# Block transposes on VectorE in a scan and in the experts, and a reordered projection stage, in a two-block network kernel

## The chip, the cores and the metric

The kernel runs on one core of a Trainium2 chip. The metric is the device time of one execution in microseconds (us); lower is better. Everything is float32. The instruction queues of TensorE (PE), ScalarE (ACT), VectorE (DVE), GpSimd (POOL, idle here) and SyncE (SP, which issues all DMAs) run side by side, each in order, and wait for each other by semaphores.

## What is computed

Two networks in a row on 256 tokens of width 1024, with 256 context tokens beside them. Cut to what the change touches:

```python
# first block, layer 0: an RWKV-7 scan over context and latent tokens, both directions
def step(S, inp):
    r_t, w_t, k_t, v_t, a_t, b_t = inp
    sa = jnp.einsum('bhvk,bhk->bhv', S, a_t)
    S = S * w_t[:, :, None, :] + sa[..., None] * b_t[:, :, None, :] + v_t[..., None] * k_t[:, :, None, :]
    return S, jnp.einsum('bhvk,bhk->bhv', S, r_t)

# first block, layer 1: 8 experts of width 2816, the best two for each token
for e in range(N_EXPERTS):
    out = out + gates[..., e:e + 1] * _swiglu(h, w1[e], w3[e], w2[e])

# second block, layer 0: gated short convolution beside differential attention
p = u @ w_in[j]                                  # gb, gc, v (512 each), q, k, v (512 each)
q, k = rope_2d(...), rope_2d(...); v = heads_v(p[..., V0:])
kvc = uc @ w_in[j][:, K0:]                       # the context's keys and values
o = diff_attention_blocks(q, concat([k, kc]), concat([v, vc]), lam)
y = jnp.concatenate([gb * short_conv(gc * v), sub_ln(o, subln_g[j], lam_init)], -1) @ w_out_mix[j]
```

The rest (Mamba scan, SwiGLU, neighbourhood attention, Fourier mixing, squared-ReLU MLPs, norms) is computed as well and is not changed.

## The kernel before, in words

The program is written engine by engine. Each engine's function lists its instructions in order; `did(engine, name)` counts a finished step on that engine's semaphore, and `at(engine, name)` gives the count that another engine waits for. So the order of the text in each function is the order of work. Weights come in slots of 256 columns through a ring of six (L500 issues each load when PE has finished the slot six before).

A float32 matmul of 128x128 by 128xN shows in the trace as two LDWEIGHTS and two MATMUL instructions. Line 928 is a helper, `two`, that issues two matmuls; 1618 is ACT's copy helper.

**The scan** (L884 to 1064 on PE, L1724 to 1772 on ACT, L2291 to 2428 on DVE) has 16 units: two directions, four chunks of 128 tokens, two groups of four heads. Each unit inverts, for each head, a triangular 128x128 matrix. `D0` holds its transposed 16x16 diagonal blocks (half 1 of the tile ED) and `E0` the same untransposed (half 0). PE squares them (E2, E4, E8), grows the inverse by T := T + T E (T2, T4, T8), and then joins blocks of 16 into 32, 64 and 128 by three bridges: Z = (masked matrix) T, then Tm = T + T Z. Powers and inverses are kept in both orientations, halves 0 and 1 of the tiles ED and TD, because a matmul wants its left operand transposed. PE computes each half by matmuls of its own; ACT copies the powers out of PSUM, 512 columns at a time; DVE adds to the inverse, 512 columns at a time (L2357 for T2, T4, T8, L2366 for the merges). `TT1` is the other half of the first inverse. The unit's other matmuls (decays, Gram products, transposes by token, outputs, state) of unit u+1 are placed between these steps. `decays(u)` on PE waits for DVE's `("state", u - 2)`, because ACT writes the exponentials `ex` that unit u - 2 still reads.

**The experts** (L1275 to 1396 on PE) run in blocks of one expert and up to 96 tokens; the table of blocks is worked out on the device, and 8 run with these inputs. A block gathers its tokens by a matmul with a one-hot matrix (L1282: 8 row tiles by 2 token chunks, 96 columns moving), giving them as 8 tiles of 128 features by 96 tokens. The up products (L1337) work in column tiles of 32: tokens are the stationary operand, three groups of 32, and the weights move, 4 parts of 352 columns of w1 or w3 into the 4 quarters of the partitions. ACT applies SiLU (L1889), DVE multiplies (L2638) into `hid`, [32 x 4 partitions, 352]. Since hidden feature 352 t + j lies in quarter t at column j, PE transposes each group in pieces of 128, 128 and 96 columns (L1321), ACT copies them out (L1894, L1895), and the down product (L1359) runs over 24 pieces of 128, 128 and 96 rows. Its weights w2 come in loads of 128 or 96 rows of 4 KB. Between its pieces PE adds the last block's outputs (L1293), turns the gates (L1379) and gathers the next block's tokens (L1282), which ACT copies out (L1868). A ring of 14 buffers carries all weights of the experts, 32 items of 704 KB (w1, w3) and 24 of 512 or 384 KB (w2) a block; SP issues item i (L597) when PE has used item i - 14.

**The second block's projections** (L1401 to 1446 on PE). After the experts come two norms, 4 and 5. Each norm is: DVE centres, ACT squares, PE sums over features by a matmul with a constant (L631), DVE adds epsilon, ACT takes the root, DVE divides and multiplies, ACT scales. Then `product` (L666) computes 16 tiles of gb, gc, v and q for the latent tokens, then four tiles of keys (L1426) for all 512 tokens, context and latent, and eight of values (L1438), each after a wait for ACT's copy of the one two before. PE turns q and k (L1415) for the rotary embedding, DVE applies it (L2674 to 2677).

**The attention** (L1448 to 1486, DVE L2682 to 2698) has eight units of a head and half of the queries. PE's order: scores of unit w+1, turned weights of w, values of w-1.

## Time and profile before

| | us |
|---|---|
| median of 3 runs | 3295.44 (3293.47 to 3298.66) |
| profiled execution, its own time | 3293.41 |
| its span | 3291.6 |
| PE busy | 3116.3 (95%) |
| DVE busy | 1283.0 (39%) |
| ACT busy | 588.3 (18%) |
| DMA | 551.15 MB, mean 167 GB/s |

The profiled execution's own time is 1.8 us more than its span, and 2.0 us less than the median. Busy times are unions over an engine's instructions. A stage can be bound by another engine than the whole, so the table is only a start: the rows below go stage by stage.

### The profile page before, as it was taken

Reading aid. Unit: us, or ns where it says so; the run is one execution under the profiler, and the core shown is the slowest. Engines: PE = TensorE matmul, PEld = TensorE weight load, DVE = VectorE, ACT = ScalarE, POOL = GpSimd, SP = SyncE. Lnnn points to the kernel's source line nnn. Section 1 sums busy time; section 2 is a strip of 40 time slices with the busy share of each in tenths; the row PEclk is TensorE's granted clock in tenths of the full one; section 3 lists DMA queues with packets and bytes.
Section 4 is the critical chain, followed back from the end, with each engine's and each line's share of the span. In section 5 each row is a group of like instructions: output and inputs, shape, how many; then the busy total and the mean of one; then the engine's idle time right before and its main releaser. Section 6 shows DMA issues by size and latency. Waiting matters only on the chain.

```text
span 3291.6 us, 52527 instructions
## 1 busy us (share of the span) xinstructions
PE 3116.3 (95%) x22488; PEld 2069.7 (63%) x22488; DVE 1283.0 (39%) x2836; ACT 588.3 (18%) x1314; POOL 0.2 (0%) x4
## 2 busy tenths in 40 slices
PE   7999899999999999999999999999999879988998
PEld 5454799997344443457745555445557568876887
DVE  1568666666799887503410101000112232122211
ACT  2114222222211111203310110010111220012000
POOL 0000000000000000000000000000000000000000
PEclk8999999999999999999999999999999889999999
DMA  7241001001577886330189999999984114531452
GB/s 264 75 154 51 1 1 40 1 1 39 189 239 243 245 248 187 123 99 25 70 317 362 357 339 337 343 362 367 349 231 130 51 52 141 153 115 51 133 148 64
DMA packets 351595, 551.15 MB, mean 167 GB/s; under 512 B 14512, under 2 KB 292400, under 8 KB 348048
## 3 DMA queue, kind: packets, MB, share of 16 engines
q1 hardware_dynamic: 351376, 547.89, 50.2%
q8 instruction: 178, 2.92, 0.4%
q14 instruction: 41, 0.34, 0.0%
HBM read 546.80 MB, written 1.05 MB: 166 GB/s over the span
## 4 chain that ended last, share of the span: by engine, by line
PE 89%; DVE 6%; ACT 2%; DMA 2%; issue 1%; SPq 0%; DVEq 0%; ACTq 0%
PE bank L666 15%; PE bank L1337 14%; PE bank L928 9%; PE bank L1130 8%; PE bank L1359 8%; PE bank L1517 7%; PE bank L1144 3%; PE bank L631 3%; PE bank L745 3%; PE bank L1171 2%; PE bank L1075 2%; DVE mix L2079 2%; PE bank L912 1%; PE bank L1282 1%; DMA arena<-in_ada_w 1%; PE bank L1426 1%
## 5 line engine op out<-in xcount | busy, mean ns | idle before, releaser
L666 PE MATMUL bank<-a,ring 128*128 128x256 f32 (+1 forms) x1792 | 454.8, 417 | 19.0 <-ACT a L1614 12.0
L666 PEld LDWEIGHTS bank<-a,ring 128*128 128x128 f32 x1792 | 344.9, 193 | 126.5 <-issue 74.5
L2079 DVE SCALAR_TENSOR_TENSOR mix<-arena,csil,mix 128x256 f32<-128x256 f32 x1008 | 402.0, 476 | 45.6 <-ACT mix L1618 45.6
L1337 PE MATMUL bank<-ring,arena 128*32 128x352 f32 x5376 | 406.9, 461 | 2.7 <-ACT small L1876 2.7
L1337 PEld LDWEIGHTS bank<-ring,arena 128*32 128x32 f32 x5376 | 175.1, 110 | 221.4 <-issue 220.4
L1130 PE MATMUL bank<-a,ring 128*128 128x512 f32 x704 | 307.5, 596 | 6.8 <-ACT a L1614 6.8
L1130 PEld LDWEIGHTS bank<-a,ring 128*128 128x128 f32 x704 | 133.2, 191 | 179.7 <-issue 178.0
L1517 PE MATMUL bank<-arena,ring 128*128 128x256 f32 x1024 | 223.5, 379 | 1.9 <-DVE arena L2736 1.9
L1618 ACT ACTIVATE arena<-bank 128x256 f32<-128x256 f32 (+1 forms) x303 | 142.0, 473 | 451.7 <-PE bank L928 199.2
L2638 DVE TENSOR_TENSOR arena<-arena,bank 128x352 f32<-128x352 f32 x48 | 25.0, 521 | 501.3 <-ACT arena L1889 501.3
L1359 PE MATMUL bank<-ring,arena 128*32 128x256 f32 (+1 forms) x3840 | 219.0, 380 | 0.6 <-issue 0.6
L1517 PEld LDWEIGHTS bank<-arena,ring 128*128 128x128 f32 x1024 | 194.4, 190 | 29.1 <-DVE arena L2736 2.8
L928 PE MATMUL bank<-arena 128*128 128x128 f32 x1408 | 180.6, 281 | 3.1 <-DVE arena L2344 2.1
L928 PEld LDWEIGHTS bank<-arena 128*128 128x128 f32 x1408 | 166.4, 193 | 14.6 <-ACT arena L1618 6.7
L1359 PEld LDWEIGHTS bank<-ring,arena 128*32 128x32 f32 (+1 forms) x3840 | 121.9, 110 | 83.5 <-issue 9.5
L1144 PE MATMUL bank<-arena,ring 128*128 128x512 f32 x352 | 154.1, 597 | 2.1 <-DVE arena L2460 2.1
L2717 DVE TENSOR_SCALAR tmpA<-bank,mods 128x256 f32<-128x256 f32 x32 | 15.5, 484 | 288.4 <-PE bank L1517 213.9
L1144 PEld LDWEIGHTS bank<-arena,ring 128*128 128x128 f32 x352 | 67.5, 192 | 88.4 <-issue 85.5
L1567 ACT ACTIVATE mix<-a 128x256 f32<-128x256 f32 x64 | 21.8, 417 | 534.1 <-DVE a L1994 534.1
L1618 ACT ACTIVATE mix<-arena,csil 128x256 f32<-128x256 f32 x144 | 64.7, 499 | 261.6 <-DMA arena<-in_ada_w 160.6
L745 PE MATMUL bank<-a,ring 128*128 128x512 f32 (+1 forms) x224 | 99.1, 596 | 0.0
L2732 DVE TENSOR_SCALAR tmpA<-bank 128x256 f32<-128x256 f32 x64 | 27.2, 424 | 167.1 <-PE bank L666 167.1
(411 smaller groups left out, 3360.6 us busy)
## 6 DMA issues: line engine op xcount, KB each, us to landing
ring<-in_moe_w SPq DMA_DIRECT2D x224, 704.0 KB, 8.4
ring<-in_mlp_w SPq DMA_DIRECT2D x64, 1024.0 KB, 5.5
ring<-in_moe_w SPq DMA_DIRECT2D x112, 512.0 KB, 8.4
arena<-in_ada_w SPq DMA_DIRECT2D x96, 512.0 KB, 3.8
arena<-in_w_ada SPq DMA_DIRECT2D x48, 512.0 KB, 3.6
ring<-in_ffn_w SPq DMA_DIRECT2D x22, 1024.0 KB, 8.5
arena<-in_moe_w SPq DMA_DIRECT2D x32, 704.0 KB, 8.8
ring<-in_moe_w SPq DMA_DIRECT2D x48, 384.0 KB, 8.4
```

The source lines that it names most:

```text
L631: i = mm(bank[b][:, 0:tile.shape[-1]], const("mean"), tile, start=(k == 0), stop=(k == KT - 1))
L666: i = mm(bank[b][:, 0:n], ws[:, k, t * P:t * P + P], rhs[:, k, sl], start=(k == 0), stop=(k == KT - 1))
L745: i = mm(bank[RKV_BANK[n]][0:m, :], ws[:, k, n % 2 * P:n % 2 * P + m], aT[:, k, :], start=(k == 0), stop=(k == KT - 1), skip_group_check=True)
L928: i = mm(bank[b][:, o + P * m:o + P * m + P], lhs[:, m, :], rhs[:, m, :], start=True, stop=True, skip_group_check=True)
L1075: i = mm(bank[MIX_BANKS[j % 5]], ws[:, k, j % 2 * P:j % 2 * P + P], src, start=(k == 4), stop=(k == 3), skip_group_check=True)
L1130: i = mm(bank[2 * t + i_], ws[:, k, t * P:t * P + P], aT[:, k, :], start=(k == 0), stop=(k == KT - 1))
L1144: i = mm(bank[2 + n % 4], ws[:, k, :], G[:, k, :], start=(k == 0), stop=(k == FT - 1))
L1337: i = mm(b[32 * t:32 * t + 32, 0:PART], ac_[:, k, 32 * g:32 * g + 32], ws[i_][:, PART * t:PART * t + PART], start=(k == 0), stop=(k == KT ...
L1359: i = mm(bank[Y_BANKS[g]][32 * q:32 * q + 32, 0:256], gT[0:rows_, p, g, o + 32 * t:o + 32 * t + 32], ws[0:rows_, 256 * q:256 * q + 256], s ...
L1517: j = mm(bank[4 + n % 2][:, 0:TL], ws[:, k, :], G2[:, 16 * half + k, :], start=(half + k == 0), stop=(half * k == 15))
L1618: act(dst, src, ACT.Copy, scale=scale).then_inc(act_done, did(AC, name))
L2079: ins = V.scalar_tensor_tensor(dst, x, cond, dst, ALU.mult, ALU.add)
```

## The change

It touches four stages.

1. In the scan, PE computes half 0 only of E2 and E4 (the powers), of T2, T4, T8 and of the first merge. DVE makes half 1 by a transpose in blocks of 32x32 (`V.transpose`), which for matrices that are zero outside their 32x32 diagonal blocks is the whole transpose. The second merge makes both halves, the third half 1, as before. `TT1` goes. The wait of `decays` for the state moves from PE to ACT and is for `("state 1", u - 2)`. DVE's order of the products, masks and additions changes.
2. In the experts, the columns of w1 and w3 are dealt to the four quarters in runs of 32: quarter t takes columns 128 c + 32 t + j. Then a 32x32 block transpose of `hid` by DVE gives features 128 c to 128 c + 127 on the partitions, and the down product has 22 pieces of 128 rows (`DOWN`). The gather puts tokens on partitions in quarters, with the features moving in runs of 32 as well, and DVE block-transposes it into `ac_`. PE's transposes of `hid` and ACT's copies of them and of the gather go. The ring has 54 items a block; the first 12 items of a block wait for the item 12 before them, not 14.
3. After the experts, the context's keys and values are computed by PE before, between and after the two norm sums of stage 5; the weights of keys and values are the first four slots (`kv2`). The latent ones follow, then gc, v, q, gb.
4. In the attention, scores run two units ahead, and the product with gb follows in DVE's first units.

```diff
-PIECES = ((0, 128), (128, 128), (256, 96))
-BLOCKS_AT = [(p, t, i) for p in range(2) for t in range(4) for i in range(3)]
-ITEMS = 32 + len(BLOCKS_AT)
+DOWN = [(p, c) for p in range(2) for c in range(PART // 32)]
+ITEMS = 32 + len(DOWN)
+def uses(i):
+    return len(range(i % MRING, ITEMS, MRING))
...
-    add("in2", w["w_in_2"][0], 0, KT, by(0, 3072))
+    add("kv2", w["w_in_2"][0], 0, KT, by(2048, 1024))
+    add("in2", w["w_in_2"][0], 0, KT, by(512, 1536) + by(0, 512))
...
-                            prev = (i - MRING) % ITEMS
+                            prev = i - MRING if i >= MRING else i + MRING * (uses(i) - 1)
...
# PE, scan
             def decays(u):
-                if u >= 2:
-                    pe.wait_ge(vec_done, at(VE, ("state", u - 2)))
...
             def grams(u):
                 pe.wait_ge(act_done, at(AC, ("bkt", u)))
+                pe.wait_ge(vec_done, at(VE, ("ar r", u)))
...
+            def squared(name, u, p, i):
+                two(POWER_BANK[p], 0, half_of(ED, i, p, 1), half_of(ED, i, p, 0)
+                    ).then_inc(pe_done, did(PE, (name, u, p)))
+            def grown(name, u, p, by, i, halves=(0,)):
+                t_ = half_of(TD, i, p, 0)
+                for half in halves:
+                    ins = two(GROW_BANK[p], 256 * half, *((t_, by) if half else (by, t_)))
...
+                grown(("Tm", lv), u, p, z, 1 - lv % 2, ((0,), (0, 1), (1,))[lv])
...
                     grown("T2", u, p, half_of(ED, 1, p, 0), 0)
+                    pe.wait_ge(vec_done, at(VE, ("E2 turned", u, p)))
                     squared("E4", u, p, 1)
...
                     grown("T4", u, p, half_of(ED, 0, p, 0), 1)
+                    pe.wait_ge(vec_done, at(VE, ("E4 turned", u, p)))
+                    squared("E8", u, p, 0)
...
# PE, experts
+            def by_tile(x, t):
+                return x.rearrange("p (c t j) -> p c t j", t=4, j=32)[:, :, t, :]
             def gather():
+                for g in range(GROUPS_OF):
                     for c in range(2):
+                        for q in range(4):
+                            i = mm(bank[4 * (g // 2)][32 * q:32 * q + 32, 256 * (g % 2):256 * (g % 2) + 256],
+                                   pm[:, c, 32 * g:32 * g + 32], by_tile(atok[:, c, :], q),
+                                   start=(c == 0), stop=(c == 1), skip_group_check=True)
...
-                                    i = mm(b[32 * t:32 * t + 32, 0:PART], ac_[:, k, 32 * g:32 * g + 32],
-                                           ws[i_][:, PART * t:PART * t + PART], start=(k == 0),
+                                    i = mm(b[32 * t:32 * t + 32, 0:PART], ac_[:, g, 32 * k:32 * k + 32],
+                                           by_tile(ws[i_], t), start=(k == 0),
...
+                for n, (p, c) in enumerate(DOWN):
...
+                                   gT[:, p, g, 32 * c:32 * c + 32],
+                                   ws[:, 256 * q:256 * q + 256], start=(n == 0),
...
# PE, second block
+            pe.wait_ge(act_done, at(AC, ("norm", 13, KT - 1, 0)))
+            context_keys(0)
+            context_keys(1)
             mean_after(5, 4)
+            context_keys(2)
             squares_in(5, LAT)
+            context_keys(3)
+            context_values(0)
+            context_values(1)
...
             scores2(0)
+            scores2(1)
             for w_ in range(len(DIFF_UNITS)):
+                if w_ + 2 < len(DIFF_UNITS):
+                    scores2(w_ + 2)
...
# ACT
             def decays(u):
+                if u >= 2:
+                    ac.wait_ge(vec_done, at(VE, ("state 1", u - 2)))
...
+                    copy((name, u, p), ED[i][:, p, 0:256], bank[POWER_BANK[p]][:, 0:256])
...
# DVE
+            def power_turned(name, u, p, i):
+                ve.wait_ge(act_done, at(AC, (name, u, p)))
+                V.transpose(ED[i][:, p, 256:512], ED[i][:, p, 0:256]
+                            ).then_inc(vec_done, did(VE, (name + " turned", u, p)))
             def grown(name, u, p, i, before):
+                V.tensor_tensor(TD[1 - i][:, p, 0:256], TD[i][:, p, 0:256], bank[GROW_BANK[p]][:, 0:256], ALU.add
...
+            def inverse_turned(name, u, p, i, before):
+                ve.wait_ge(vec_done, before)
+                V.transpose(TD[i][:, p, 256:512], TD[i][:, p, 0:256]).then_inc(vec_done, did(VE, name))
...
+                grown("T2", u, 0, 0, at(VE, ("T1", u)))
+                power_turned("E4", u, 0, 0)
...
+                grown("T4", u, 0, 1, at(VE, ("T2", u, 0)))
+                grown("T4", u, 1, 1, at(VE, ("T2", u, 1)))
...
+                    inverse_turned(("T8 turned", u, p), u, p, 1, at(VE, ("T8", u, p)))
...
+                    inverse_turned(("Tm turned", u, 0, p), u, p, 0, at(VE, ("Tm", u, 0, p)))
...
+            def gathered(g, inc, counter, name):
+                V.transpose(ac_[:, g, :], bank[4 * (g // 2)][:, 256 * (g % 2):256 * (g % 2) + 256]
+                            ).then_inc(inc, did(counter, (name, g)))
...
+                def hidden_turned(p, g):
+                    ve.wait_ge(ve_moe, e * per + at(VEM, ("hid", p, g)))
+                    V.transpose(gT[:, p, g, :], hid[:, p, g, :]).then_inc(ve_moe, did(VEM, ("gT", p, g)))
...
+                if 1 <= w_ < 5:
+                    gated_conv(w_ - 1)
```

## Rows read from the trace of the kernel before

**Rows 1.** The page's chain that ended last, by engine.

```profile
PE 89%; DVE 6%; ACT 2%; DMA 2%; issue 1%; SPq 0%; DVEq 0%; ACTq 0%
```

**Rows 2.** Windows: span, busy per engine (instructions), PE clock, DMA share, GB/s.

```profile
346.00:795.00 449.00, 437.10 (x3657) 411.42 (x3658) 285.94 (x543) 123.30 (x298) 0.00 (x0) 1.00 0.03 11
1857.00:1957.00 100.00, 100.00 (x1468) 51.72 (x1460) 8.40 (x22) 10.02 (x26) 0.00 (x0) 1.00 1.01 352
...
2600.00:2650.00 50.00, 30.38 (x128) 21.33 (x128) 19.37 (x45) 21.17 (x59) 0.00 (x0) 0.76 0.07 21
```

**Rows 3.** Windows: one unit of the scan (PE, PEld, DVE, ACT, POOL).

```profile
374.00:402.00 28.00, 27.19 (x231) 25.55 (x230) 18.28 (x35) 7.80 (x19) 0.00 (x0) 1.00 0.00 1
```

**Rows 4.** Timeline of the scan: start, us, engine, line, operation, shapes.

```profile
455.46 0.68 DVE L2340 TENSOR_TENSOR arena<-arena,consts 128x512 f32<-128x512 f32 x1
...
456.66 0.87 DVE L2366 TENSOR_TENSOR ring<-arena,bank 128x256 f32<-128x256 f32 x2 [0.52 <-PE bank L928]
...
457.44 0.68 DVE L2344 TENSOR_TENSOR arena<-arena,consts 128x512 f32<-128x512 f32 x1
...
465.64 0.69 DVE L2357 TENSOR_TENSOR arena<-ring,bank 128x512 f32<-128x512 f32 x1 [2.22 <-PE bank L928]
...
467.02 3.65 PEld L928 LDWEIGHTS bank<-arena 128*128 128x128 f32 x32
```

**Rows 5.** Waits in the scan: who for whom, us in total, times, longest.

```profile
PE bank L891 <- DVE ring L2424: 5.8, 8, 0.7
...
PE bank L891 <- DVE ring L2426: 4.3, 6, 0.7
```

**Rows 6.** Timeline of norm 4: DVE's reciprocal.

```profile
2465.26 1.75 DVE L2009 RECIPROCAL tmpA<-tmpB 128x256 f32<-128x256 f32 x1 [0.48 <-ACT tmpB L1580]
```

**Rows 7.** Chain of waits in the experts: start, us, what, instructions.

```profile
1698.44 0.48 PE bank L1321 x3
...
1745.80 3.74 PE bank L1282 x32
1749.54 9.21 PE bank L1359 x168
1758.75 39.05 PE bank L1337 x528
...
1957.47 2.64 PE bank L1337 x33
```

**Rows 8.** Windows: w2 alone loading, then w1 and w3 alone; DMA share, GB/s last.

```profile
1920.00:1940.00 20.00, 20.00 (x354) 12.21 (x350) 3.23 (x8) 1.50 (x6) 0.00 (x0) 1.00 1.02 287
1950.00:1990.00 40.00, 40.00 (x584) 18.91 (x580) 2.04 (x5) 3.61 (x7) 0.00 (x0) 1.00 1.01 406
```

**Rows 9.** DMA issues from 1920 to 1940: count, size, median us to landing.

```profile
ring<-in_moe_w SPq DMA_DIRECT2D x4, 512.0 KB, 8.7
ring<-in_moe_w SPq DMA_DIRECT2D x2, 384.0 KB, 8.3
```

**Rows 10.** Waits of SP's queue in the experts.

```profile
SPq L597 <- PE bank L1337: 351.8, 128, 22.3
```

**Rows 11.** Chain of waits from norm 4 to the last values.

```profile
2460.51 3.73 PE bank L631 x16
...
2468.07 6.25 PE bank L631 x16
...
2585.57 13.83 PE bank L1438 x64
2599.43 0.38 ACT arena L1618
```

**Rows 12.** Chain of waits over one unit of the attention.

```profile
2620.91 1.29 DVE small L2685 x2
...
2623.37 1.12 PE bank L737 x4
...
2627.62 1.29 DVE small L2685 x2
```

More of the change, by code:

```diff
@@ new lines, in context_values @@
+            def context_values(c):
+                for half in range(2):
+                    ws = full(first["kv2"] + 2 + half)
+                    for k in range(KT):
+                        i = mm(bank[5 - c][:, 256 * half:256 * half + 256], aT[:, k, c * P:c * P + P],
+                               ws[:, k, :], start=(k == 0), stop=(k == KT - 1), skip_group_check=True)
+                i.then_inc(pe_done, did(PE, ("v2 ctx", c)))
+            pe.wait_ge(act_done, at(AC, ("norm", 13, KT - 1, 0)))
@@ L1416, in turn @@
                    ).then_inc(pe_done, did(PE, ("turn", n)))
[L1418 to L1419 removed]
+            for j in range(4):
+                s = first["kv2"] + j // 2
                 ws = full(s)
[L1421 to L1429 removed]
@@ L1430, in _ @@
[L1430 to L1443 removed]
+                if j >= 2:
+                    pe.wait_ge(act_done, at(AC, ("k2", j - 2)))
@@ new lines, in _ @@
+                for k in range(KT):
+                    if j == 0:
+                        normed(5, k)
+                    i = mm(bank[2 + j % 2][:, 0:TL], ws[:, k, j % 2 * P:j % 2 * P + P], aT[:, k, LAT],
+                           start=(k == 0), stop=(k == KT - 1))
+                i.then_inc(pe_done, did(PE, ("k2", j), *([("slot", s)] if j % 2 else [])))
+            for n in range(4):
+                half, c = n // 2, 2 + n % 2
+                s = first["kv2"] + 2 + half
+                ws = full(s)
+                pe.wait_ge(act_done, at(AC, ("v2 ctx", n) if n < 2 else ("v2", n - 2)))
+                for k in range(KT):
+                    i = mm(bank[5 - n % 2][:, 0:256], aT[:, k, c * P:c * P + P], ws[:, k, :],
+                           start=(k == 0), stop=(k == KT - 1))
+                i.then_inc(pe_done, did(PE, ("v2", n), *([("slot", s)] if c == 3 else [])))
+                turn(n)
@@ L1444, in _ @@
+            pe.wait_ge(act_done, at(AC, ("k2", 3)))
+            product("in2", first["in2"], 8, aT, LAT, [2, 3],
+                    lambda j: pe.wait_ge(act_done, at(AC, ("in2", j))),
+                    then=lambda j: turn(j - 4) if 8 <= j < 12 else None)
+            pe.wait_ge(act_done, at(AC, ("in2", 15)))
             pe.wait_ge(vec_done, at(VE, ("rope", 7)))
-            pe.wait_ge(act_done, at(AC, ("v2", 7)))
             def scores2(w_):
```

266 lines of the change are left out of this document (110 added, 156 removed).

## The prediction

> **What bounds it now.** I read the chain of waits first: PE's work makes 89% of it [rows 1], so what counts is where PE is busy, and whether it would stay busy with less to do. The table of stages answers by stage [rows 2]. In the RWKV scan (346 to 795 us) PE is busy 437 of 449 us while DVE is busy 286: PE-bound. In a middle stretch of the experts it is busy 100 of 100 us, but the DMA share is 1.01 too, so two resources are full and taking work from one may show the other. In the attention of the second block (2600 to 2650) PE is busy 30 of 50 us at a granted clock of 0.76: a chain of waits, not work. The profiled execution took 3293.4 us, 2.0 under the median of the three runs shown; the sums below go against it, and 2 us are added at the end.
>
> **The scan.** One unit takes 28.0 us, with PE busy 27.2 of them [rows 3]; there are 16. The change keeps only one orientation of most small inverses on PE and lets DVE turn it in 32x32 blocks. Per unit it drops these 128x128 matmuls: E2 4, E4 4, T2, T4 and T8 4 each, first merge 4; 24 in all. Each is two instructions in the trace, and 32 instructions in a row take 3.65 us [rows 4], 0.114 each; 48 x 0.114 = 5.5 us a unit, -87.5 us over 16. The decays no longer wait for the state of u-2 on PE (ACT waits for the earlier "state 1" instead); that wait is 5.8 + 4.3 us [rows 5]: -10.
>
> What DVE gets: 8 transposes of 128x256 a unit. No row shows one. Its lower bound is nothing (a transpose cannot free DVE); for the upper I take the slowest 128x256 operation of DVE, the reciprocal at 1.75 us [rows 6]. I take 0.45, nearest to the 128x256 additions, which write as many elements (0.87 us for two) [rows 4]. DVE also gives back: six additions and two merges shrink from 512 to 256 columns (0.69 to 0.43, 2.1 us) and the 512-wide "TT1" goes (0.7). So DVE gets 3.6 and loses 2.8 us: some 18.7 busy in a unit of 22, and ACT's four 512-wide copies become 256 wide. The reordered products of DVE (bh and kh first, then ar) have the same work; the Gram products now also wait for "ar r", which is issued after both T4 additions and before T8: about 0.1 us more. The chain of each step gets longer while PE has less to fill it: T2's addition plus E4's transpose on DVE is about 0.9 us against two pairs of PE products of 0.45 each, so T4 of the second pair comes 0.1 to 0.2 late. The three bridges wait for ACT as before. I add 0.3 us a unit, +5. Sum of the scan -93; a unit of about 22.1 us. With transposes at 0.9 us, 8 x (0.9 - 0.6) comes onto the unit, since beyond about 0.6 each one lies on the chain: then the scan gives -64.
>
> **The experts.** There are 8 blocks, the second and third taking (1957.47 - 1758.75) / 2 = 99.4 us each [rows 7]. Off PE in each: six groups of transposes of the hidden values at 0.48 = 2.9 us; two of the 24 pieces of the down product, since 96-row pieces go (seven pieces take 9.21, so 1.32 each): 2.6; the gather goes from 3.74 us to 24 matmuls of 256 columns in four column tiles, which is what two down pieces are, 2.6: 1.1 less [rows 7]. Together 6.6 us a block; PE alone would want 92.8. DVE gets nine transposes a block beside 8.4 us of work in 100 [rows 2]: hidden, with PE's own products as cover (the last is wanted 11 pieces later). ACT loses its copies. The first block starts later, since its three transposes follow "blocks" on DVE: +1.
>
> The moving operand of all up products is now read in 11 runs of 32 columns, 512 bytes apart. No row of PE shows such a read. On DVE, a read in four runs of 128 columns costs 0.68 us (L2340), as the unbroken L2344 does [rows 4]. I take nothing; the bound above is half the rate, which is a rival below. The page Advanced Engine Details and Errata of the Trainium skill (Memory Cachelines) gives SBUF lines of 16 bytes and no penalty within one, which a run of 128 bytes keeps; its rule that any non-contiguous pattern slows matmuls significantly is about PSUM, which the change still writes contiguously.
>
> But the DMA: while only w2 is loaded it moves 287 GB/s at a share of 1.02, and while only w1 and w3 are, 406 at 1.01 [rows 8]. A block needs 32 x 721 KB = 23.1 MB and 11.5 MB, so 56.8 + 40.2 = 97.0 us if these rates are the DMA's own. If w2's time goes by transfers and not by bytes, 22 for 24, it is 56.8 + 36.8 = 93.6. For the latter speaks that 384 KB take as long to land as 512 KB (8.3 and 8.7) [rows 9]; against a DMA bound, that SP waited 352 us for the up products to free slots [rows 10]. I take 94.2, so 5.2 a block and -42 in all; ends 92.8 and 97.0, -53 and -19. The page DMA: Bandwidth & Descriptors of the Trainium skill (Specifications) gives about 358 GB/s of HBM for a core, and a block of 34.6 MB would take 96.7 us by it; the 406 GB/s over 40 us speak against that as a limit here.
>
> **The second block's projections.** From the norm sum of stage 4 (2460.51 + 3.73 = 2464.2) to the end of v2 (2599.43) are 135.2 us [rows 11]. PE's work in them is that of two norm sums (2 x 3.45), and, at the 13.83 us that v2 takes for 64 instructions, 55.3 for in2's 256 and 27.7 each for keys and values, eight turns, two instructions each (3.5): 121.1. The change moves no work off PE; it puts the context's half of keys and values, 27.7 us, into the gaps between the norms, with its weights as the first four slots, of which six 1 MB loads begin when the experts end. The norms themselves then come some 3 us later, but behind them lie 17 us of keys and values that need none of them. So the stage becomes pure PE work, 14.1 shorter; a stretch at the lower clock of 1.2 GHz, which before took 6.25 us for 16 instructions [rows 11], will probably cost some 2 us somewhere: -12 (-8 to -14). The gated product with gb moves behind the scores; DVE has the room.
>
> **The attention.** A unit takes 2627.62 - 2620.91 = 6.7 us, all in series: DVE's maxima, ratio and weights 2.5 us, then PE's turn, values and the next scores, 4.2 us from 2623.37 [rows 12]. With scores two ahead, the scores and maxima leave that chain. What remains is the larger of PE's own 4.2, most of it at the lower clock (half of it at the full one), and ACT's and DVE's 2.5 to 3; I take 4.7 with its waits. Over seven periods, -14 (-8 to -17).
>
> **Sum.** -93 - 42 + 1 - 12 - 14 = -160: 3133.4, and on the median 3135.
>
> **Rivals.**
> **DMA-bound experts**: blocks of 97.0 us instead of 94.2 give back 8 x 2.8 = 22: 3157. For it, the share of 1.01; against, SP's waits for PE. 20%.
> **Slow transposes**: at 1.3 us instead of 0.45, DVE's chain adds 8 x 0.7 = 5.6 us to a unit, 90 in all: 3225; at 1.75 the whole scan gives nothing. 8%.
> **Moving runs, the other side**: the four column tiles make 192 quad passes a block, at 0.296 us each (39.05 us for 528 instructions, 132 passes) [rows 7], 1536 in all. If a run of 32 columns makes PE read at half rate, each takes 0.30 more: +450, some 3585. It decides from 160 / 1536 = 0.10 us more a pass, 35%: then the change is slower than before. By the PSUM rule above, were it true of moving reads, it would come out here; nothing in the trace speaks for it. 7%.
> **Latency under the PE work**: the scan does not follow its work, since the chain of products, ACT copies and DVE additions already took 28 us. Then only the experts, the projections and the attention gain: 3228. Against it, DVE waited for PE and not the reverse, and PE idles only 0.8 us of a unit [rows 3]. 5%.
> My forecast, with its pieces a little off: 60%.
>
> **The numbers.** Predicted 3135. Below, all ends at their best (-96, -53, -14, -17) give 3116, with a little for a faster clock in the attention 3108. Above, the DMA-bound case and transposes near 0.9 give 3135 + 22 + 29 = 3186; I stop at 3190 and leave out the slow transposes beyond that, the latency and the moving runs. Under 0.2%, about 7 us, a measurement cannot tell a change from none. Faster 0.91, the same 0.02, slower 0.07, from the moving-runs case.
>
> **What would show it.** A scan unit near 22 us with PE still busy over 95% (else the chain is the bound), a transpose row near 0.45 us; up products still at 39 us for 528 instructions; blocks of 93 to 95 us, and PE waits for a DMA in the experts if the DMA is the bound; no idle of PE between 2464 and the scores; attention units under 5 us. The forecast is wrong if the up products' passes take over 0.31 us, or if the scan's unit stays over 24.

## The result and the profile after

The kernel after takes **3103.97 us** (median of 4 runs, 3100.58 to 3104.77), the kernel before on the same chip 3294.99 (3293.47 to 3298.66): a ratio of 0.9417, 95% interval 0.9400 to 0.9433. The change gives 191 us where the prediction said 160. The direction was right; the time lies 4 us below the low end of the range (3108). So the prediction is wrong in size, and the question is which terms were too small.

The profiled execution took 3104.1 us, its span 3102.3. Cut at the same places in the chain of waits of both kernels (start of the up products of the first block, end of the experts' last down piece, end of the projections, start of the output product), the 189.3 us between the spans are:

| stage | before | after | difference | forecast |
|---|---|---|---|---|
| up to the experts' start | 1657.63 | 1562.16 | -95.5 | -93 + 1 |
| eight blocks of experts | 798.0 | 736.9 | -61.0 | -42 |
| norms and projections | 143.8 | 129.6 | -14.2 | -12 |
| attention | 54.9 | 33.6 | -21.2 | -14 |
| the rest | 637.3 | 639.9 | +2.6 | 0 |

The two terms that are off are the experts' (19 us) and the attention's (7 us).

**The scan.** A window of the kernel after, as long as a unit (columns: stretch, its length, busy time and instructions of PE, PEld, DVE, ACT and POOL, granted clock, DMA share, GB/s; against [rows 3]):

```profile
374.00:396.00 22.00, 21.92 (x184) 20.36 (x183) 18.22 (x42) 6.92 (x19) 0.00 (x0) 1.00 0.00 1
```

and two of its three groups of DVE's block transposes in the scan (count, busy us, mean ns, then the idle time before them; the third, 32 of the inverse in other buffers, has 445 ns):

```profile
L2357 DVE STREAM_TRANSPOSE arena<-arena 128x256 f32<-128x256 f32 x64 | 28.3, 443 | 12.6 <-ACT arena L1628 12.3
L2370 DVE STREAM_TRANSPOSE arena<-arena 128x256 f32<-128x256 f32 x32 | 14.3, 446 | 1.1
```

A transpose takes 0.44 us (0.45 was taken), and a unit 22.0 us (22.1 was forecast). What the reader should see is PE at 21.92 of 22.00: the unit is still nothing but PE's work, and DVE, to which the transposes went, has 18.2 us of work in a unit, as before.

**The experts.** The chain of waits of the kernel after through one block (start, duration, what; it stands against [rows 7]):

```profile
1656.59 56.80 PE bank L1336 x768
1713.39 10.36 PE bank L1352 x192
1723.75 2.80 PE bank L1295 x48
1726.56 9.20 PE bank L1352 x168
...
1736.56 2.73 PE bank L1352 x48
1739.29 2.59 PE bank L1284 x48
1741.88 6.47 PE bank L1352 x120
1748.36 56.80 PE bank L1336 x768
```

A block takes 1748.36 - 1656.59 = 91.77 us, all PE, where the forecast had 94.2 and its floor, PE alone, 92.8. The DMA did not hold it up. Its windows after, the whole stretch in which only rows of w2 move and a stretch in which only w1 and w3 do, and its landings of w2 (KB each, median us from issue to landing), against [rows 8, 9]:

```profile
1791.00:1823.00 32.00, 32.00 (x520) 17.47 (x516) 6.12 (x14) 1.39 (x3) 0.00 (x0) 1.00 0.91 344
1842.00:1862.00 20.00, 20.00 (x276) 8.78 (x272) 0.00 (x0) 0.42 (x1) 0.00 (x0) 1.00 1.02 418
```
```profile
ring<-in_moe_w SPq DMA_DIRECT2D x160, 512.0 KB, 6.6
```

w1 and w3 come at the old rate (418 GB/s, 406 before). w2 comes at 344 GB/s where the prediction read 287, and at a lower share, 0.91 for 1.02. The window of that reading holds the ends of w1 and w3 as well, by some 5% of its rows; over the whole stretch in which only rows of w2 moved, the kernel before had this:

```profile
1899.00:1937.00 38.00, 38.00 (x579) 19.83 (x575) 4.79 (x11) 4.12 (x13) 0.00 (x0) 1.00 1.01 276
```

That is the surprise: the same weights, from the same place, a quarter faster, and nothing in the change was seen as touching their rate. By the new rates a block's weights need 23.1 MB / 418 GB/s + 11.5 MB / 344 GB/s = 55.2 + 33.5 = 88.7 us (an estimate from these windows), 3 us less than PE's 91.8.

**The projections.** The chain after: from the norm sum (L634) to the end of gb (L669) PE's pieces follow each other without a gap.

```profile
2304.11 3.72 PE bank L634 x16
2307.83 6.91 PE bank L1395 x32
...
2328.55 13.81 PE bank L1405 x64
...
2418.34 10.37 PE bank L669 x48
```

Its window, with PE busy all but 0.1 us and the granted clock at 1.00:

```profile
2304.00:2428.00 124.00, 123.89 (x574) 109.04 (x575) 31.48 (x75) 25.97 (x62) 0.00 (x0) 1.00 0.42 135
```

**The attention.** One steady unit of the chain after, and the start of the next, against [rows 12]:

```profile
2444.74 0.66 PE bank L740 x4
2445.39 0.89 PE bank L1481 x8
2446.29 1.06 PE bank L1462 x4
...
2447.38 0.66 PE bank L740 x4
```

A unit takes 2447.38 - 2444.74 = 2.64 us, all PE. It took 6.7 before, and 4.7 was forecast. PE's three pieces, turn, values and scores, are 2.6 us here and were 1.12 + 1.71 + 1.40 = 4.2 before. The granted clock (third column from the right) was 0.76 there [rows 2]; here it is low only in the first units, behind 6 us (2428 to 2434) of which PE was busy 4.0:

```profile
2434.00:2442.00 8.00, 7.86 (x28) 4.42 (x27) 6.06 (x14) 4.47 (x13) 0.00 (x0) 0.57 0.00 0
2442.00:2450.00 8.00, 7.66 (x49) 4.88 (x49) 7.52 (x17) 6.62 (x22) 0.00 (x0) 1.00 0.00 1
```

So these are the same instructions at the upper clock of 2.4 GHz instead of mostly at the lower one.

### The profile page after: what moved, and what is told of

The parts are those of the page before. It is cut to its first block, busy times and chain, and to the rows that moved or that the text cites. A ratio compares the mean times of both kernels' runs of the same rounds, so it can differ in the third digit from the quotient of the medians.

```text
span 3102.3 us, 50418 instructions
## 1 busy us (share of the span) xinstructions
PE 2959.7 (95%) x21400; PEld 1945.2 (63%) x21400; DVE 1316.5 (42%) x3023; ACT 539.0 (17%) x1200; POOL 0.2 (0%) x4
## 4 chain that ended last, share of the span: by engine, by line
PE 90%; DVE 5%; ACT 2%; DMA 2%; issue 1%; SPq 0%; DVEq 0%; ACTq 0%
PE bank L669 16%; PE bank L1336 15%; PE bank L1128 9%; PE bank L1352 7%; PE bank L1527 7%; PE bank L930 7%; PE bank L1142 4%; PE bank L634 3%; PE bank L748 3%; PE bank L1169 2%; PE bank L1073 2%; DVE mix L2083 2%; PE bank L914 1%; DMA arena<-in_ada_w 1%; PE bank L1203 1%; PE bank L1295 1%
## 5 line engine op out<-in xcount | busy, mean ns | idle before, releaser
L669 PE MATMUL bank<-a,ring 128*128 128x256 f32 (+1 forms) x1792 | 453.4, 415 | 15.4 <-ACT a L1624 8.3
L669 PEld LDWEIGHTS bank<-a,ring 128*128 128x128 f32 x1792 | 343.6, 193 | 121.9 <-issue 70.2
L1336 PEld LDWEIGHTS bank<-ring,arena 128*32 128x32 f32 x5376 | 176.4, 110 | 227.9 <-issue 226.9
L1352 PE MATMUL bank<-ring,arena 128*32 128x256 f32 x3840 | 213.3, 379 | 0.0
L1628 ACT ACTIVATE arena<-bank 128x256 f32<-128x256 f32 (+1 forms) x303 | 127.7, 428 | 371.6 <-PE bank L930 137.3
L1352 PEld LDWEIGHTS bank<-ring,arena 128*32 128x32 f32 x3840 | 124.2, 110 | 83.4 <-issue 4.0
L930 PE MATMUL bank<-arena 128*128 128x128 f32 x896 | 125.4, 285 | 3.9 <-DVE arena L2350 2.1
L930 PEld LDWEIGHTS bank<-arena 128*128 128x128 f32 x896 | 110.1, 193 | 16.5 <-ACT arena L1628 7.7
L748 PE MATMUL bank<-a,ring 128*128 128x512 f32 (+1 forms) x224 | 99.6, 599 | 0.0
```

What stands on the lines that cost most here:

```text
L669: i = mm(bank[b][:, 0:n], ws[:, k, t * P:t * P + P], rhs[:, k, sl], start=(k == 0), stop=(k == KT - 1))
L748: i = mm(bank[RKV_BANK[n]][0:m, :], ws[:, k, n % 2 * P:n % 2 * P + m], aT[:, k, :], start=(k == 0), stop=(k == KT - 1), skip_group_check=True)
L930: i = mm(bank[b][:, o + P * m:o + P * m + P], lhs[:, m, :], rhs[:, m, :], start=True, stop=True, skip_group_check=True)
L1336: i = mm(b[32 * t:32 * t + 32, 0:PART], ac_[:, g, 32 * k:32 * k + 32], by_tile(ws[i_], t), start=(k == 0), stop=(k == KT - 1), skip_group_ ...
L1352: i = mm(bank[Y_BANKS[g]][32 * q:32 * q + 32, 0:256], gT[:, p, g, 32 * c:32 * c + 32], ws[:, 256 * q:256 * q + 256], start=(n == 0), stop= ...
L1628: act(dst, src, ACT.Copy, scale=scale).then_inc(act_done, did(AC, name))
```

## The experiments

### Each part alone

Four kernels, each the kernel before with one of the four parts of the change and nothing else. Their cores:

```diff
# scan alone
-                    ins = two(POWER_BANK[p], 256, e, d_)
+                V.transpose(ED[i][:, p, 256:512], ED[i][:, p, 0:256]
# experts alone
-PIECES = ((0, 128), (128, 128), (256, 96))
+DOWN = [(p, c) for p in range(2) for c in range(PART // 32)]
# projections alone
+            context_keys(0)
+            context_keys(1)
             mean_after(5, 4)
# attention alone
             scores2(0)
+            scores2(1)
```

> The kernel before with the scan's part of the change alone. By the stages of the two traces the scan gave 96.6 us. If the parts are independent this gives -95 to -98 against before, ratio 0.970 to 0.971. If the scan's gain owes something to the other parts (the clock, say), less. My forecast for the term was -93.

> The kernel before with the experts' part alone. The stages gave -61.1 in the experts and +1.1 before them; forecast -42, with ends -53 and -19. If the parts are independent: -58 to -62, ratio about 0.982, blocks of 91.8 us. If the experts' extra gain came from elsewhere (the scan or the projections feeding the weights' queue), -42 to -53 and blocks of 93 to 94.

> The kernel before with the second block's projections reordered alone. The stages gave -14.1; forecast -12 (-8 to -14). Independent parts: -12 to -15. Rival: the product with gb, moved into the attention, costs there when scores run only one unit ahead: then -6 to -10. Nothing else should move.

> The kernel before with the scores of the attention two units ahead, alone. The stages gave -21.2; forecast -14 (-8 to -17), with units of 4.7 us. After the change the units take 2.65 us at the full clock. Theory one, the clock came back because the scores ahead keep PE busy: then -19 to -22 here too. Theory two, the full clock came from the unbroken PE work of the projections ahead of it: then only -12 to -17 here, with units of 4 to 5 us at a granted clock under 0.9.

| run | median us | ratio to before (95%) | against 3297.15 |
|---|---|---|---|
| scan alone | 3198.96 | 0.9697 (0.9671 to 0.9722) | -98.2 |
| experts alone | 3237.35 | 0.9814 (0.9788 to 0.9841) | -59.8 |
| projections alone | 3283.58 | 0.9960 (0.9940 to 0.9980) | -13.6 |
| attention alone | 3269.88 | 0.9912 (0.9886 to 0.9938) | -27.3 |

The kernel before ran from 3291.9 to 3311.0 in this job, so each difference is good to some 8 us. They add up to 199, the change to 191: the parts are independent within that. The experts' gain is their own, with the landing of w2 at 6.5 us in that kernel too, so neither the scan nor the other order of slots made w2 faster.

The attention's 27.3 against the 21.2 of its stage lies within that. Its trace tells which theory holds. Between 2600 and 2650 us, where the kernel before has PE busy 30.38 us at a clock of 0.76 [rows 2], it shows:

```profile
2600.00:2650.00 50.00, 42.11 (x207) 30.40 (x206) 22.98 (x53) 23.14 (x64) 0.00 (x0) 0.90 0.07 22
```

and its chain has a unit of 2.55 us:

```profile
2619.59 0.59 PE bank L737 x4
...
2622.14 0.62 PE bank L737 x4
```

The stage, from the end of v2 to the output product, takes 2640.12 - 2607.72 = 32.4 us, 22.5 less than before. The projections ahead of it are the old ones here, and in the projections alone, whose PE work runs into the attention without a gap, the units keep the old pieces (1.12, 1.71 and 1.2 to 1.5 us). So the clock came back because scores two ahead keep PE busy in the attention, as theory one said, not because of what runs ahead of it.

### The wait of the decays

```diff
             def decays(u):
-                if u >= 2:
-                    pe.wait_ge(vec_done, at(VE, ("state", u - 2)))
-                elif u == 0:
+                if u == 0:
# ACT, before it writes the exponentials
+                if u >= 2:
+                    ac.wait_ge(vec_done, at(VE, ("state 1", u - 2)))
```

> The kernel before, with only the wait of the decays for the state of u-2 taken from PE, and ACT waiting for the earlier state 1 of u-2 before it writes the exponentials. My term for it was -10: the 5.8 and 4.3 us that PE waited for DVE there. If that wait is worth its length, -8 to -10, ratio about 0.997. Rival: the steps behind it wait instead (for the bridges' masks and copies), since PE gets to them earlier: then -2 to +2, and the whole -96 of the scan is from the fewer matmuls.

It takes 3282.59 us, ratio 0.9957 (0.9941 to 0.9972): 13.9 us less. The rows of the decays' line in the kernel before, in this one, in the one with doubled transposes (next section) and in the kernel after, in that order, give the scan's pace (duration min/median/max, then start of the first and last instruction, one set of four a unit):

```profile
L891 PE MATMUL bank<-consts,ring x64: 381/381/576, 332.4 to 748.4; 128*128 128x258 f32 x64
```
```profile
L889 PE MATMUL bank<-consts,ring x64: 381/381/639, 335.0 to 737.5; 128*128 128x258 f32 x64
```
```profile
L892 PE MATMUL bank<-consts,ring x64: 381/381/639, 335.6 to 690.2; 128*128 128x258 f32 x64
```
```profile
L892 PE MATMUL bank<-consts,ring x64: 381/381/639, 333.9 to 661.9; 128*128 128x258 f32 x64
```

The decays of unit u+1 open unit u, so from the first to the last lie the scan's opening and fourteen whole units: 416.0, 402.5, 354.6 and 328.0 us. PE's busy time in these stretches, of the kernel before, of this one and of the kernel after:

```profile
332.40:748.40 416.00, 397.77 (x3300) 372.37 (x3301) 265.15 (x507) 112.44 (x274) 0.00 (x0) 0.98 0.03 9
```
```profile
335.00:737.50 402.50, 394.43 (x3299) 371.26 (x3300) 265.13 (x507) 112.38 (x273) 0.00 (x0) 0.99 0.03 9
```
```profile
333.90:661.90 328.00, 320.61 (x2620) 296.43 (x2621) 267.35 (x608) 99.99 (x273) 0.00 (x0) 0.98 0.03 11
```

The wait was worth 13.5 us: PE idles 10.2 us less, the wait's own length, and the same matmuls take 3.3 us less, at a mean granted clock of 0.99 for 0.98. Nothing took its place, and the rival is out. The other 402.5 - 328.0 = 74.5 us are the matmuls that were dropped: PE is busy 73.8 us less, 5.3 a unit, and its idle time went from 8.1 to 7.4. So the transposes put no wait in PE's way that shows here, where the prediction had set 5 us aside.

### Each transpose twice

```diff
                 ve.wait_ge(vec_done, before)
+                op(("once", name), V.transpose(TD[i][:, p, 256:512], TD[i][:, p, 0:256]))
                 V.transpose(TD[i][:, p, 256:512], TD[i][:, p, 0:256]).then_inc(vec_done, did(VE, name))
```

and the same for the powers.

> The kernel after, with each of the scan's eight block transposes a unit done twice, one after the other (0.44 us each in the profile after). It measures how much room the chain of a unit has under PE's work. My prediction held that a transpose has about 0.6 us before it lies on the chain, and 0.9 us would cost 8 x 0.3 = 2.4 us a unit, +38 us. A model of the unit with each engine's queue in order gives 23.7 us for a unit of 22.0, +27. If PE's work covers the transposes well: under +10. DVE's busy time goes from 18.2 to 21.7 us a unit, so DVE itself is then nearly full.

3133.81 us (3129.17 to 3137.72) against 3103.40 for the kernel after in the same job: +30, of which the rows above show 354.6 - 328.0 = 26.6 in fourteen units, 1.9 a unit. Eight more transposes are 8 x 0.446 = 3.6 us a unit, so half of their time comes onto the path. The model of the queues (+27) came close, the rule of the prediction (room up to 0.6 us, then all of it, +38) was too harsh. The waits of PE in this kernel show where (us in total, times, longest):

```profile
PE bank L930 <- DVE ring L2372: 7.7, 16, 0.5
PE bank L930 <- DVE arena L2365: 6.7, 15, 1.3
```

L2372 is the transpose of the inverse after T8 or the first merge, L2365 the addition to the inverse. In the kernel after, the same view shows one PE wait of 0.6 us for that addition (L2364) and one of 0.4 for that transpose (L2370) in all of the scan: a transpose of 0.44 us just fits.

### The moving operand in runs of 32

```diff
-                                           by_tile(ws[i_], t), start=(k == 0),
+                                           ws[i_][:, PART * t:PART * t + PART], start=(k == 0),
```

> The kernel after, with the moving operand of the up products read in one run of 352 columns, as before, instead of 11 runs of 32 (hidden features land in other places, so the values differ). If runs of 32 columns cost nothing, the up products of a block stay at 56.8 us (768 instructions) and the whole within 3 us of after. If they cost something, the block falls by it: 0.01 us a pass would be 1.9 us a block and 15 us in all.

3097.15 us in one run. The up products and the block, from its chain:

```profile
1745.33 56.80 PE bank L1336 x768
...
1837.09 7.97 PE bank L1336 x105
```

56.80 us for 768 instructions and a block of 91.76, both the same to 0.01 us as with runs of 32. Moving runs of 32 float32 columns, 512 bytes apart, cost nothing, and almost all of the 7 us between the two totals lies ahead of and behind the experts, in the spread of single runs (the kernel after itself ran from 3096.85 to 3106.20 in another job).

### Why w2 became faster

Three kernels for three theories: the loads of 96 rows slow the whole stream (A), it is where the rows start (B), or the rate is that of the bytes and bounds the block (C). The kernels of this section and the next read other rows of w2 than the network wants or leave old ones in the slots, so they show times only, and each is one run. In the kernel before:

```diff
-                                f0 = MCOLS * p + PART * t + o
-                                src = w["moe_w2"][0][one, f0:f0 + n, :]
-                                dst = dst[0:n, 0:D]
+                                f0 = MCOLS * p + PART * t + o + n - P
+                                src = w["moe_w2"][0][one, f0:f0 + P, :]
+                                dst = dst[:, 0:D]
```

> The kernel before, with every load of w2 128 rows long: where it read the last 96 rows of a piece, it now reads the 128 rows that end there (the down product of that piece still multiplies 96 partitions, with values of other rows). w2's bytes grow by 9%. Before, w2's loads took 8.4 us from issue to landing, and while only they ran the DMA share was 1.02 at 287 GB/s; after the change 6.6 us, 0.85 and 317 GB/s. Theory A, the 96-row loads slow the whole stream of w2: landings fall to about 6.6 to 7 us, the share in a w2-only window to 0.9 or less at 310 GB/s or more. Theory B, it is where the rows start (before at multiples of 32 rows, after at multiples of 128): landings stay at 8.4 us or grow, share 1.0. Theory C, the rate is that of the bytes, and the DMA bounds the block: the block grows from 99.4 us to 102 or more. By A and B, PE bounds the block before: it stays at 99.4 us, and the whole within 5 us of before.

In the kernel after, with loads of 96 rows back, 6 of 22 where 8 of 24 were, and with all loads shifted:

```diff
-                                src = w["moe_w2"][0][one, f0:f0 + P, :]
-                                dst = dst[:, 0:D]
+                                n = 96 if c % 3 == 2 else P
+                                src = w["moe_w2"][0][one, f0:f0 + n, :]
+                                dst = dst[0:n, 0:D]
# the shifted one
-                                f0 = MCOLS * p + P * c
+                                f0 = MCOLS * p + P * c + (32 if c < 10 else 0)
```

> The kernel after, with every third load of w2 96 rows instead of 128 (the last 32 rows of those slots keep what lay there; the products are as many). PE's work is unchanged, w2's bytes fall by 8%. Theory A (96-row loads slow the stream): landings of w2 rise from 6.6 to 8 us or more and the share in a w2-only window from 0.85 to 0.95 or more, with fewer bytes moved. Whether the block of 91.8 us grows is open: if the DMA then needs more than that, it goes to 93 to 95. Theory B (the start of the rows): landings stay at 6.6 us and the share falls to about 0.8.

> The kernel after, with w2's rows read 32 rows later (still 128 rows a load; ten of eleven loads multiply other rows than they should). Theory A (96-row loads): as after, landings 6.6 us, share 0.85, block 91.8 us. Theory B (loads that start at a multiple of 128 rows, 512 KB, are faster): landings 8 us or more, share 0.95 or more.

3294.43 us (before, all loads 128 rows), **3126.51** (after, every third load 96 rows) and 3105.45 (after, shifted). The stretches in which only rows of w2 move, and the landings, first of the kernel before with 128 rows:

```profile
1899.00:1938.00 39.00, 39.00 (x593) 20.34 (x587) 4.79 (x11) 4.27 (x14) 0.00 (x0) 1.00 0.87 303
```
```profile
ring<-in_moe_w SPq DMA_DIRECT2D x160, 512.0 KB, 5.5
```

then of the kernel after with every third load 96 rows:

```profile
1794.00:1826.00 32.00, 32.00 (x531) 19.70 (x527) 6.12 (x14) 1.39 (x3) 0.00 (x0) 1.00 1.03 259
```
```profile
ring<-in_moe_w SPq DMA_DIRECT2D x120, 512.0 KB, 20.0
ring<-in_moe_w SPq DMA_DIRECT2D x40, 384.0 KB, 20.0
```

Theory A holds from both sides. With 9% more bytes, the kernel before moves w2 at 303 GB/s instead of 276, at a share of 0.87 instead of 1.01, and lands a load in 5.5 us instead of 8.4. With 7% fewer bytes, the kernel after moves it at 259 instead of 344, and lands a load in 20.0 us instead of 6.6. B is out: shifted rows land in 6.6 us and cost nothing. C, the byte rate as the bound, is out as well, since the larger w2 left the block at 99.4 us.

The second of the three is also what the prediction's reading would have looked like in time. Its chain has the loads in it (the time of an entry is a load's whole flight, not a wait), here in the fifth block, between the start of the first up products and the end of the last down piece:

```profile
1560.58 59.50 PE bank L1337 x768
...
1983.82 23.13 DMA ring<-in_moe_w
...
2318.04 6.52 PE bank L1353 x120
```

From 1655 to 2243 us PE is busy 573.5 of 588 us there, and all 588 in the kernel after. The eight blocks take 2324.56 - 1560.58 = 764.0 us where the kernel after takes 736.9: 27 us more, of which the whole shows 22 (the stretches outside differ by 5, within the spread of single runs). The loss grows as the lead of the ring is used up. From one start of the up products to the next are 94.4, 92.8, 94.1, 94.0, 99.3, 96.4 and 96.2 us (94.3 and then 91.8 or 91.9 in the kernel after), and the last four blocks take 97.2 on the mean. By this kernel's own rates a block needs 10.7 MB / 259 GB/s + 23.1 MB / 418 GB/s = 96.7 us (an estimate). So the sum of the two rates is what a block takes once the DMA is the bound: the prediction's 97.0, and not the 94.2 that it took.

### What makes a short load slow

```diff
+                                n = 64 if c % 3 == 2 else P      # or 112; or n = 96 for all
```

> The kernel after, with every third load of w2 64 rows instead of 128. With 96 rows there the time went from 3104 to 3126.5 us, the w2-only window from 317 GB/s at a share of 0.85 to 265 at 1.03, and 512 KB took 20.0 us to land instead of 6.6. Theory P, 96 rows are slow because they don't divide evenly (six rows for each of the 16 DMA engines, where 128 rows give eight and 64 give four): with 64 rows the time stays within 3 us of 3104, the share in a w2-only window at 0.7 to 0.8, landings near 6.6 us. Theory Q, any mixture of lengths disturbs the stream, or any load under 128 rows is slow: 3115 us or more, landings over 10 us, share over 0.95.

> The kernel after, with every third load of w2 112 rows (seven for each DMA engine). Theory P: slow as with 96, 3115 us or more, landings over 10 us. Theory Q with the loss growing with what is missing from 128: about half of the 22 us of 96 rows, 3110 to 3118. If 112 rows cost nothing (3104, landings 6.6), it is 96 alone that is slow.

> The kernel after, with every load of w2 96 rows. The bytes of w2 fall to three quarters. If a load of 96 rows is slow by itself (P), the stream stays slow: 3115 us or more, the w2-only window under 270 GB/s at a share over 1. If it is the alternation of 96 and 128 that is slow (part of Q), it recovers: 3104 us, the w2-only window at a share of 0.65 to 0.8 and landings under 6.6 us.

| w2 in the kernel after | whole, us | eight blocks | GB/s, share | one row |
|---|---|---|---|---|
| all 128 rows | 3103.97 | 736.9 | 344, 0.91 | 0.17 us |
| every third 64 | 3105.06 | 741.0 | 264, 1.03 | 0.26 |
| every third 96 | 3126.51 | 764.0 | 259, 1.03 | 0.26 |
| every third 112 | 3146.87 | 779.6 | 270, 1.03 | 0.25 |
| all 96 | 3105.93 | 745.5 | 247, 1.02 | 0.27 |

The eight blocks are cut as in the table of stages. The rates are of the stretches in which only rows of w2 move: 1791 to 1823, 1790 to 1822, 1794 to 1826, 1805 to 1833 and 1790 to 1822 us. The last column is an estimate of how long one of the 16 DMA engines is busy with a row of 4 KB: the share times 16 times the stretch, over the packets of 512 B and more. (The expectations quote shorter windows, 317 GB/s at 0.85 for all 128 rows and 265 at 1.03 for every third 96.) Two of the windows, 112 and all 96:

```profile
1805.00:1833.00 28.00, 24.62 (x412) 14.04 (x408) 6.12 (x14) 1.39 (x3) 0.00 (x0) 1.00 1.03 270
```
```profile
1790.00:1822.00 32.00, 31.53 (x511) 18.91 (x507) 6.13 (x14) 1.39 (x3) 0.00 (x0) 1.00 1.02 247
```

and the packets of the first row of the table and of the third:

```profile
DMA packets 3015, 11.00 MB, mean 344 GB/s; under 512 B 341, under 2 KB 341, under 8 KB 3011
```
```profile
DMA packets 2282, 8.30 MB, mean 259 GB/s; under 512 B 269, under 2 KB 269, under 8 KB 2278
```

Neither theory comes out. P had 64 rows harmless: the whole is unchanged, but the share is 1.03, the landings are 9.9 us and the blocks take 4 us more. Q had all 96 recover: the rate stays at 247 GB/s, and the whole hardly moves because a quarter of the bytes is gone (the blocks take 9 us more even so). What the runs do show is simpler and enough for the case. With full loads alone a row takes a DMA engine 0.91 x 16 x 32 / 2674 = 0.17 us; as soon as 64, 96 or 112 rows stand in every third load, or 96 in all, it takes 0.25 to 0.27 on the mean. The rows of the full loads are among the slow ones: with every third load 96 rows, 22% of the rows belong to short loads, but the median of all rows from 1650 to 2290 us, in the trace's own records of packets, is 0.236 us, and 0.159 in the kernel after. The kernel before fits as well, with 0.24 us a row and 0.19 once all its loads have 128 rows. So leaving out 32 rows of every third load, or even 16, costs 22 and 43 us. The page DMA: Bandwidth & Descriptors of the Trainium skill (Why a DMA increments its semaphore by 16 and not by 1) says that 96 rows are spread over as many of the DMA engines, 16, as 128; a full share with 96 rows agrees with that, and so the loss isn't from idle engines. Why each row gets slower is left open, and so is why 112 rows cost more than 96 at about the same rate.

### The first block earlier

An attempt at a faster version. In the trace after, the first gather ends on PE at 1557.2 us, but DVE turns the tokens only behind its small operations:

```profile
1552.02 5.20 PE L1284 MATMUL bank<-arena 128*32 128x256 f32 x48 [1.33 <-DVE arena L2592]
1560.60 1.11 DVE L2634 STREAM_TRANSPOSE arena<-bank 128x256 f32<-128x256 f32 x3
1562.16 4.33 PE L1336 MATMUL bank<-ring,arena 128*32 128x352 f32 x28 [4.94 <-DVE small L2642]
```

```diff
# DVE: ahead of the operations that lead to "blocks", not behind them
+            ve.wait_ge(pe_done, at(PE, "gather first"))
+            for g in range(GROUPS_OF):
+                gathered(g, vec_done, VE, "gathered first")
+            ve.wait_ge(vec_done, now(VE))
+            V.memset(small[:, 701:702], 0.0).then_inc(ve_moe, per)
             which4 = which.rearrange("p i (m e) -> p i m e", m=2)
# ACT: releases the block before it waits for "blocks"
-            act(small[:, 700:701], small[:, 604:605], ACT.Copy).then_inc(ac_moe, per)
+            act(small[:, 700:701], small[:, 32:33], ACT.Copy).then_inc(ac_moe, per)
+            ac.wait_ge(vec_done, at(VE, "blocks"))
```

> The kernel after, with the first block of experts let go earlier. In the trace after, the first gather ends on PE at 1557.2 us, but DVE turns it only at 1560.6, behind the small operations that work out which experts need a second block, and PE starts the up products at 1562.2. None of those small operations is needed by the first block's up products. Here DVE turns the gathered tokens ahead of them, right when the gather ends, and releases PE and ACT then. Expected: the up products start at 1558.6, 3.5 us earlier, and the whole is 3 to 4 us faster (ratio to after 0.9989). Rivals: ACT, which must now load its table and wait for the number of blocks, is late for the first SiLU (it is wanted 27 us later, so no); or the later small operations delay the first mask of gathered tokens (wanted at the end of the block, so no): then nothing is gained.

> The kernel after once more, beside the next one on the same chip: 3100 to 3105 us.

```profile
1550.25 4.48 PE L1284 MATMUL bank<-arena 128*32 128x256 f32 x48 [1.32 <-ACT a L1624]
1555.30 1.11 DVE L2617 STREAM_TRANSPOSE arena<-bank 128x256 f32<-128x256 f32 x3
1556.87 9.59 PE L1336 MATMUL bank<-ring,arena 128*32 128x352 f32 x104 [2.13 <-DVE small L2625]
```

From the start of the gather to the first up product are 10.1 us in the kernel after and 6.6 here: 3.5 less, as expected. The runs took 3097.66 us (3097.32 to 3101.34) against 3103.40 (3096.85 to 3106.20). Their ratios to before, 0.9400 (0.9388 to 0.9413) and 0.9407 (0.9394 to 0.9420), overlap, so of the 5.7 us between the medians only the 3.5 in the trace is shown. (A second trace of the kernel after has the same 10.1 us, from 1553.10 to 1563.24.)

## Why the prediction was right in direction and wrong in size

- **The scan, -93 and measured -96.6** (95.5 to the experts' start, with 1.1 given back there). The count of dropped matmuls held, a transpose cost 0.44 us, and PE stayed at 99.6% of a unit. The size is partly luck, since three terms were off and nearly cancelled: the dropped matmuls gave 5.3 us a unit, some 84 in all, for 87.5 (the price of 0.114 was read from a row of weight loads); the decays' wait gave 13.5 for 10; and the 5 us set aside for new waits were not needed. Two slips in the working decide nothing here: DVE's terms add up to 19.1 us a unit and not 18.7 (measured 18.2), and transposes at 0.9 us cost 38 us by the rule given, so that the scan would have given -55 and not -64, and the upper sum 3195.
- **The experts, -42 and measured -61.0.** This is the step that failed: "if these rates are the DMA's own". I took 287 GB/s at a full share for w2's rate, and so 94.2 us a block, between PE's own 92.8 and 97.0 by the two rates. The rate belonged to a stream with 96-row loads in it, which the change takes away; w2 came at 344 GB/s, and PE was never held up. I had the observation that 384 KB take as long to land as 512 KB, and drew from it only that time goes by transfers; not that the short loads could be what slows the full ones. The twin run with 96 rows shows that the resource was rightly suspected: without that side effect the blocks would have cost 27 us more, with 97.2 us each in the last four, which is the DMA-bound rival's block. Of the 19 us between -42 and -61, 11 are this hold-up that did not come (94.2 to 92.8).
- **PE's own share of it** was undersized as well, and makes the other 8. The forecast had 6.6 us a block. By the chains: turns 2.9 (as forecast), down products 31.92 - 28.76 = 3.2 (2.6), gather 3.74 - 2.59 = 1.15 (1.1), up products 57.22 - 56.80 = 0.4 (nothing, since three turns stood between them before). Together 7.6, 1.0 a block more than forecast. So even the end that I called PE alone, -53, was not the end.
- **The projections, -12 and measured -14.2.** The stretch at the lower clock that I had set 2 us aside for did not come: from 2304 to 2428 us the granted clock is 1.00.
- **The attention, -14 and measured -21.2.** The chain broke up as foreseen, and PE's own work became the bound. I priced that work "most of it at the lower clock", from rows in which PE idled 40% of the time; but the change takes that idling away, and with it the lower clock. A unit is 2.6 us, the bound at the full clock (4.7 was taken).
- **The rest** gave back 2.6 us; the output product after the attention took 10.07 us for its 32 instructions where it took 8.74. The granted clock is 0.71 from 2462 to 2473 us, and was 0.81 over the same product before; that is 1.3 of the 2.6 us, and the cause of the other half is open.
- **The rivals**: slow transposes, slow moving runs and latency under the PE work are all out, each by a run or a row, and the DMA-bound one did not come true, with blocks of 91.8 us and PE never waiting. The range was too narrow below. Its low end already left the DMA out; what it lacked was PE's own share of the experts (8 us more than its -53) and the attention at the upper clock (4 us more than its -17), against 8 us kept for the clock.

## What to carry to other kernels

A rate read at a full share is the rate of that mix of transfers, not of the hardware: before it goes into a floor, ask whether the change alters the mix, and keep all loads of a stream at 128 partitions, even if the last rows are loaded twice (here this gave w2 in the kernel before 303 GB/s for 276; the time stayed, since PE set the pace). In the same way a duration read at a low clock holds only as long as the idling that caused it; where a change makes the engine busy, price the work at both clocks and take the upper one if the forecast itself says that the gaps go (this case has one such stage). DVE's 32x32 block transpose is worth having where a matrix is zero outside its diagonal blocks, or where the order of features can be chosen so that blocks suffice: it took PE work off at no cost as long as one transpose fits in the slack between two of PE's steps.

## What the runs showed of the hardware

- A float32 block transpose on DVE takes 443 to 446 ns for 128x256 within SBUF, 421 ns on the mean from PSUM in the experts (27 of them), and 526 ns for 128x352 (48).
- Loads of 64, 96 or 112 rows among loads of 128 take a stream of 4 KB rows from 344 GB/s (0.91 share) to 264, 259 and 270 (1.03), though they carry fewer bytes; 96 rows in every load give 247 (1.02).
- The DMA moved 418 GB/s in a stretch of w1 and w3 in the kernel after. The page DMA: Bandwidth & Descriptors of the Trainium skill (Specifications) puts the limit of HBM for one core at about 358 GB/s, as half of what two cores share; the measured 418 speaks against that as a limit where one core runs.
- Reading the moving operand in 11 runs of 32 float32 columns is as fast as in one run of 352: 56.80 us for 768 instructions either way.
